# Casting weight loads one by one, replicated tables, and moved gating in a hybrid encoder kernel on eight cores

## What is computed

```python
def layer(x, c, ...):
    mod = jax.nn.silu(c) @ w_ada + b_ada                    # (B, 3D)
    shift, scale, gate = jnp.split(mod, 3, axis=-1)
    h = rmsnorm(x, norm_g) * (1.0 + scale[:, None, :]) + shift[:, None, :]
    z = h @ w_in                                            # (B, S, IN_WIDTH)
    a, ga, u, v, gb, ma, mb = jnp.split(z, IN_SPLITS, axis=-1)
    y_a = fourier_branch(a, w_fmix, b_fmix) * jax.nn.silu(ga)
    y_b = sgu_branch(u, v, sgu_ln_g, sgu_ln_b, w_s, b_s) * jax.nn.silu(gb)
    merged = jax.nn.sigmoid(ma) * (y_a @ w_pa) + jax.nn.sigmoid(mb) * (y_b @ w_pb)
    out = merged @ w_out
    return x + gate[:, None, :] * out
```

## Time and profile before

| what | value |
|---|---|
| median of 3 runs | 1265.08 us (1264.58 to 1265.36) |
| profiled execution | 1264.34 us |
| its span on the slowest core (core 4) | 1262.8 us |
| spans of the eight cores | 1249.7 to 1262.8 us |
| granted TensorE clock, mean per core | 0.984 to 0.991 of full |
| TensorE busy | 1203.5 us, 95% of the span |
| VectorE (DVE), ScalarE (ACT), GpSimd (POOL) busy | 700.2, 474.9, 318.8 us |

### The profile page before, as it was taken

The page is one execution under the profiler, slowest core; times in us unless marked ns, Lnnn a source line. Parts: engine busy times, 40 slices in busy tenths (PEclk is TensorE's granted clock), DMA queues, the critical chain, the costliest instruction groups (busy, mean ns, idle before and its releaser), DMA issues.

```text
span 1262.8 us, 19703 instructions; the slowest of 8 cores (1249.7 to 1262.8 us)
## 1 busy us (share of the span) xinstructions
PE 1203.5 (95%) x6128; PEld 564.2 (45%) x6128; DVE 700.2 (55%) x1133; ACT 474.9 (38%) x818; POOL 318.8 (25%) x406
## 2 busy tenths in 40 slices
PE   5799689999999999998999999999998999999997
PEld 0254344444444455545444444444443444444443
DVE  0384285554857668857556355445554663564544
ACT  1384232233323458845423432334232333332322
POOL 0131022461131232201721311312225413122111
PEclk9899899999999999999999999999999999999999
DMA  8999696325465278844430331413326315124121
GB/s 272 257 256 149 169 156 145 100 84 167 138 178 195 75 239 270 272 148 128 97 110 24 109 110 62 138 42 96 97 76 141 122 45 145 59 83 118 51 84 67
DMA packets 91123, 166.59 MB, mean 132 GB/s; under 512 B 39818, under 2 KB 52490, under 8 KB 89870
## 3 DMA queue, kind: packets, MB, share of 16 engines
q1 hardware_dynamic: 80606, 138.98, 35.4%
q0 software_dynamic: 9120, 17.96, 9.5%
q10 hardware_dynamic: 1296, 8.40, 2.0%
HBM read 143.41 MB, written 31.47 MB: 138 GB/s over the span
## 4 chain that ended last, share of the span: by engine, by line
PE 86%; DMA 8%; DVE 2%; POOL 1%; issue 1%; ACT 1%; ACTq 0%; SPq 0%; POOLq 0%; DVEq 0%
PE ps L702 43%; PE ps L621 13%; PE ps L814 6%; PE ps L820 6%; PE ps L505 6%; PE ps L712 5%; DMA arena<-w_ada 3%; DMA arena<-Gd 2%; PE ps L462 2%; DMA arena<-xA 1%; PE ps L515 1%; DMA Gd<-arena 1%; DMA arena<-xB 1%; PE ps L758 1%; PE ps L780 1%
## 5 line engine op out<-in xcount | busy, mean ns | idle before, releaser
L702 PE MATMUL ps<-arena 128*128 128x512 bf16 x2688 | 606.9, 381 | 5.4 <-ACT arena L806 3.5
L702 PEld LDWEIGHTS ps<-arena 128*128 128x128 bf16 x2688 | 262.7, 98 | 321.6 <-issue 16.5
L806 ACT ACTIVATE arena<-ps 128x512 bf16<-128x512 f32 x192 | 112.1, 595 | 243.4 <-PE ps L702 203.9
L825 POOL TENSOR_TENSOR arena<-arena 128x512 bf16<-128x512 bf16 x84 | 112.7, 1341 | 295.5 <-DVE arena L823 295.4
L621 PE MATMUL ps<-arena 128*128 128x512 bf16 x768 | 171.3, 379 | 0.4 <-DVE arena L823 0.4
L817 DVE TENSOR_TENSOR arena<-ps,arena 128x512 bf16<-128x512 f32 x96 | 66.2, 690 | 189.9 <-PE ps L814 187.5
L635 ACT ACTIVATE arena<-arena 128x1024 bf16<-128x1024 f32 x48 | 50.7, 1057 | 217.8 <-DVE arena L631 217.7
L408 POOL TENSOR_TENSOR stat<-stat,eps_sb 128x1 f32<-128x1 f32 (+1 forms) x114 | 28.8, 253 | 391.4 <-ACT arena L635 290.4
L421 ACT ACTIVATE arena<-arena 128x1024 bf16<-128x1024 f32 x96 | 101.3, 1055 | 69.0 <-DMA arena<-xB 45.5
L427 DVE TENSOR_SCALAR arena<-arena,stat 128x1024 bf16<-128x1024 f32 x96 | 84.7, 909 | 69.3 <-POOL stat L410 69.1
L621 PEld LDWEIGHTS ps<-arena 128*128 128x128 bf16 x768 | 75.1, 98 | 91.1 <-issue 1.5
(11 more groups left out here) (76 smaller groups left out, 930.6 us busy)
## 6 DMA issues: line engine op xcount, KB each, us to landing
arena<-xB SPq DMA_DIRECT2D x96, 512.0 KB, 4.5
arena<-xA SPq DMA_DIRECT2D x48, 512.0 KB, 6.8
yu<-arena SPq DMA_DIRECT2D x48, 512.0 KB, 2.8
arena<-w_ada SPq DMA_DIRECT2D x24, 512.0 KB, 5.2
arena<-w_in POOLq DMA_DIRECT2D x9, 1024.0 KB, 16.4
arena<-w_ada ACTq DMA_DIRECT2D x8, 1024.0 KB, 23.9
Gd<-arena SPq DMA_DIRECT2D x48, 128.0 KB, 5.4
arena<-Gd SPq DMA_DIRECT2D x12, 512.0 KB, 8.6
```

The source lines that it names most:

```text
L702: S.pe([lambda e, kc=kc: e.matmul(ps[b][:], lhsT=w_in_sb[:, sec, kc, col:col + 128], rhs=tb.hT[:, kc, :], start=(kc == 0), stop=(kc == 7)) ...
L806: S.op("act", lambda e, b=b, so=so: e.activation(out=bv(so, 512), in_=ps[b][:], func=AF.Sigmoid), reads=[("ps", b)], writes=gk(so, 1024))
L825: S.op("pool" if dmc < 7 else "dve", lambda e: e.tensor_tensor(out=tb.mg[:, dmc, :], in0=tb.mg[:, dmc, :], in1=bv(sl[1], 512), op=ALU.add) ...
```

## The change

1. `w_sec(0)` waits for chunk 5 of `w_ada` in place of 6, and the loads of x chunks 4 to 7 for chunk 6 in place of 7. In the first pass `sc(3)` moves behind the first projection's cast. The last `stage1` of a pass (`flush`) moves behind the next tile's transposes (first pass) or behind the first V group of tile 4 (second pass).
2. Sections 3 and 5 leave `hooks1`: section 3 is issued after V of tile 0, section 5 after GB of tile 0, `w_pab` after GB of tile 1, section 7 after U of tile 1. To say "after", the matmul groups now also write a key `("sec", sec)` that the casting DMA reads.
3. `b_adaG`, `ln_b`, `b_s` and `final_g` come as 128 equal rows in memory in place of one row that is read 128 times. `s3_begin(1)` comes ahead of `late_tabs`.
4. `sgu` moves behind `ga_section` in tiles 0, 1 and 4; `z_tr(1, ..)` of tile 5 moves from GA to GB; `w_out`'s products alternate between POOL and DVE and start one round later.
5. The very last `out_chunk` takes squares, scaling and store in halves of 512 columns.

```diff
@@ start and casts
-    w_sec(0, after=gk(wada_off[6], 512))
+    w_sec(0, after=gk(wada_off[5], 512))
...
-        3: lambda: (w_sec(4, after=[("aq", 1, 15)]), w_s_load(), w_sec(3), w_sec(5)),
+        3: lambda: (w_sec(4, after=[("aq", 1, 15)]), w_s_load()),
...
-    A.load_to(8, after=gk(wada_off[7], 512))
+    A.load_to(8, after=gk(wada_off[6], 512))
...
-    A.sc(3)
-    A.body(hooks1)
+    A.body(hooks1, late=True)
@@ groups
     def fm_group(tb, sec, col):
...
-             reads=gk(tb.h, 8192) + wink[sec], writes=[("ps", b)])
+             reads=gk(tb.h, 8192) + wink[sec], writes=[("ps", b), ("sec", sec)])
...
-                 reads=gk(tb.h, 8192) + wink[SEC["V"]], writes=[("ps", b)])
+                 reads=gk(tb.h, 8192) + wink[SEC["V"]], writes=[("ps", b), ("sec", SEC["V"])])
@@ tiles 0 and 1
+    A.fe(5)
+    A.flush()
+    s3_begin(1)
     late_tabs()
-    s3_begin(1)
-    A.fe(5)
-    for tb in pair:
-        v_section(tb)
+    v_section(T0)
+    w_sec(3, after=[("sec", SEC["V"])])
+    v_section(TB1)
     silu_section(T0, SEC["GB"], T0.sgb, T0.b)
+    w_sec(5, after=[("sec", SEC["GB"])])
     silu_section(TB1, SEC["GB"], TB1.sgb, TB1.b, lambda fc: s3s(0) if fc == 3 else None)
+    w_pab()
     u_section(T0, lambda fc: s3s(1 + fc // 2) if fc % 2 else None)
     channel_tables()
     w_sec(6)
-    w_pab()
-    w_sec(7)
+    u_section(TB1, lambda fc: s3s(3) if fc == 1 else None)
+    w_sec(7, after=[("sec", SEC["U"])])
     w_sec(8)
-    u_section(TB1, lambda fc: s3s(3) if fc == 1 else None)
-    for tb in pair:
-        sgu(tb)
-    w_out_load()
     final_tab()
     gate_load(0, 0)
     gate_load(1, 1)
     ga_section(T0, 0, 0, lambda fc: z_tr(1, fc))
+    sgu(T0)
     ga_section(TB1, 0, 1)
+    sgu(TB1)
+    w_out_load()
@@ products of w_out with the gate
-        S.op("pool", lambda e: e.tensor_tensor(out=w_out_sb[:, k, :], in0=w_out_sb[:, k, :], in1=fv(off, 1024), op=ALU.mult),
+        S.op(("pool", "dve")[k % 2], lambda e: e.tensor_tensor(out=w_out_sb[:, k, :], in0=w_out_sb[:, k, :], in1=fv(off, 1024), op=ALU.mult),
...
-    mul_order = ((0, 1), (2, 3), (4,), (5,), (6,), (7,), (), ())
+    mul_order = ((), (0, 1), (2, 3), (4, 5), (6, 7), (), (), ())
@@ tiles 4 and 5
-        v_section(tb)
+        v_section(tb, (lambda: (A2.flush(), s3_begin(0))) if T == 4 else None)
...
+            if T == 5:
+                z_tr(1, fc)
...
-        sgu(tb)
+        if T != 4:
+            sgu(tb)
...
-        ga_section(tb, u, t, (lambda fc: z_tr(0, fc)) if T == 4 else (lambda fc: z_tr(1, fc)) if T == 5 else None)
+        ga_section(tb, u, t, (lambda fc: z_tr(0, fc)) if T == 4 else None)
+        if T == 4:
+            sgu(tb)
@@ last chunk, in out_chunk
+            if last:
+                S.op("act", lambda e, half=half: e.activation(
+                    out=bv(O_XSR + 6144 + 1024 * half, 512), in_=xv[:, half * 512:(half + 1) * 512], func=AF.Square, scale=0.03125,
+                    accum_out=stat[:, 0, si + half:si + half + 1]),
+                    reads=hk, writes=[("st", si + half)] + gk(O_XSR + 6144 + 1024 * half, 1024))
+                if half == 0:
+                    finish()
```

More of the change, by code:

```diff
@@ L613, in finish, with out_chunk @@
             fins.pop(0)()
-    def out_chunk(tb, T, j, k, split=False):
-        si = stat2(1)
+    def out_chunk(tb, T, j, k, split=False, last=False):
+        si = stat2(2 if last else 1)
         row0 = T * 512 + j * 128
@@ L633, in out_chunk @@
                 reads=[("ps", b)] + hk, writes=hk)
+            if last:
[5 more added lines that the diff above has]
+                    finish()
+        if last:
+            S.op("dve", lambda e: e.scalar_tensor_tensor(out=stat[:, 1, si:si + 1], in0=stat[:, 0, si:si + 1], scalar=EPS,
+                                                         in1=stat[:, 0, si + 1:si + 2], op0=ALU.add, op1=ALU.add),
+                 reads=[("st", si), ("st", si + 1)], writes=[("st1", si)])
+            S.op("pool", lambda e: e.tensor_tensor(out=stat[:, 1, si:si + 1], in0=stat[:, 1, si:si + 1], in1=mh_sb[:, 0:1], op=ALU.pow),
+                 reads=[("st1", si), "mh"], writes=[("st1", si)])
+            for half in range(2):
+                hs = slice(half * 512, (half + 1) * 512)
+                hk = gk(XS[k] + 2048 * half, 2048)
+                S.op("dve", lambda e, hs=hs: e.scalar_tensor_tensor(out=xv[:, hs], in0=xv[:, hs], scalar=stat[:, 1, si:si + 1],
+                                                                    in1=fg_bc[:, hs], op0=ALU.mult, op1=ALU.mult),
+                     reads=hk + [("st1", si), "fg"], writes=hk)
+                out_tokens.append(S.dma("sp", [lambda e, hs=hs: e.dma_start(out=yu.ap()[row0:row0 + 128, hs], in_=xv[:, hs])],
+                                        "s_st%d" % (k if half else (k + 2) % 4), reads=hk, writes=[("yout", row0, half)]))
+            return
         jo = O_TYB if T in (0, 1, 3) else O_XSR + 6144
@@ L886, in body @@
                     if j % 2 == 0:
+                        if late and q == 0 and j == 0:
+                            self.sc(3)
                         self.sc(2 * q + j // 2 + 4)
```

35 lines of the change are left out of this document (18 added, 17 removed).

## The result

The kernel after takes **1272.43 us** (median of 5 runs, 1270.64 to 1273.28) against 1265.36 (5 runs, 1264.58 to 1266.77) for the kernel before on the same chip: a ratio of **1.0053**, 95% interval 1.0038 to 1.0068. That is slower by 7.1 us, where 1270 was forecast, 5 us slower. In some executions the cores of one half of the chip run at a lower granted clock and the time is longer; all medians and ratios here leave those out. The profiled execution took 1272.06 us, with a span of 1270.2 on core 4, the slowest core before too; the spans compared, 1270.2 - 1262.8, give 7.4.

The account below looks back on a forecast made before the run. TensorE bounds the kernel (86% of the chain). Terms: +15.1 to the end of U of tile 1, gating -5.4, tile 4 -1.5, tile 5 0, tile 8 -3.1: +5.1 on 1264.34, about 1270 us with the median's 0.7; range 1266 to 1275.

Parts of the forecast that it names:

- section 3: V of tile 1: TensorE waits 17.5 us for this w_in cast, landing at about 121.5; bounds 14.4 and 21.
- Section 5: GB of tile 1: TensorE waits 11.7 us for this w_in cast to land; bounds 7 and 16.4.
- The old wait: L575, after GB of tiles 0 and 1: TensorE's wait of 11.8 us for Gd goes.
- The start: First pass: earlier x loads and sc(3) behind the cast -3.3, flush behind the transposes -0.6; V of tile 0 at 97.1.
- The restarts: After TensorE's waits: 1.6 us at low clock for each, two in place of one, +1.6; bounds 0 and 3.2.
- Gating, tiles 0 and 1: Spatial gating moved beside GA and the sigmoid groups: -5.4 us, leaving 2 us for late banks; bounds -7.4 and -2.
- Tile 4: Waits of 1.28 and 1.1 us go, 0.9 is given back by the Fourier table: -1.5; bounds -2.4 and +1.
- Tile 5: Channel products moved from GA to GB: 4.2 us won, +3.9 from banks still held, net 0; bounds -4.2 and +2.
- Tile 8: Products on two engines, one round later, end TensorE's waits for sigmoids behind POOL: -3.1 us; bounds -3.5 and 0.
- The last chunk: End of the kernel: halves save 0.5 us on ACT, finish() puts a scaling ahead; 0, bounds -1 and +1.
- the fast casts: Rival, chance 0.11: awaited casts land at their queue's pace, two waits together under 21.5 us, sum 8.0 lower, 1262.
- The crowded casts: Rival, chance 0.10: section 3 lands as before less the shift (+3.5), section 5 meets other transfers (16.4, +4.8): 1278 us.

Follow-up runs that it names:

- the casts late: Kernel after, no group waiting for a cast's landing, and sections 5, 6, w_pa and w_pb called behind the channel tables: 1243.05 us, ratio 0.9826.
- the kernel with the old products: Kernel with the casts late, but w_out's products all on POOL in their old places: 1244.44 us, ratio 0.9853.
- the start alone: Kernel before with only the earlier first cast and x loads, the fourth scaling behind the cast, flush behind the transposes: 1262.99 us, ratio 0.9999.
- tiles 4 and 5 alone: Kernel before with only tile 4's Fourier first step, flush and gating moved and tile 5's channel products in GB: 1262.52 us, ratio 0.9975.
- the casts alone: Kernel before with only sections 3, 5 and 7 cast behind matmul groups, reading their key, and w_pa, w_pb behind GB of tile 1: 1290.45 us, ratio 1.0201.
- one-row tables and late casts: Kernel with the casts late, but ln_b, b_s, b_adaG and final_g again one row in memory: 1249.69 us, ratio 0.9873.

## Why the prediction was right

**The new waits.** The price of section 3 was 17.5 us, measured 16.0 on core 4 and 15.3 to 19.7 over the cores. Its landing was put at 121.5 and came at 119.2: issued 0.9 earlier than reckoned, and 13.3 us on the way, nearer to the lone cast of the earlier trace rows than to the crowded one. Section 5 was priced at 11.7 and took 12.6 (9.0 to 13.0). Here the Trainium skill's rule ("DMA: Bandwidth & Descriptors", "Anatomy of one DMA") had given an estimate of 6.8 us from issue to landing; the measured 11.84 us, with no other queue moving a packet, is against it, as the earlier trace rows was, and so are all eight cores (8.2 to 12.2). That these waits are what the change costs is shown by the kernel without them (-13 us) and by the one with the casts late (-29).

**The old wait.** Gone: the last load of `Gd` lands at 125.2 and TensorE asks for it at 155.9. The reason that the prediction gives for the old wait, the casts, is only a part of it, as the table above shows. The start gave -4.8 where -3.9 was reckoned (3.1 to the transposes, then 1.7 because the matmuls behind them run at full clock, which stood in the bounds only). The restarts cost 1.86 and 1.31 us, the old one 1.63: +1.5, forecast +1.6. The end of U of tile 1 moved by +13.5 where **+15.1** was forecast.

**Gating, tiles 0 and 1.** -5.4 forecast; -4.9 in the trace (-4.5 to -5.7 over the cores), -5.1 alone. The forecast left 2 us for banks that come free late; the rows show 1.65 and 0.25.

**Tile 4** was mis-sized, -1.5 against -4.3 (-2.5 to -4.4 over the cores, mean -3.2). The wait that was to give back 0.9 is there and is larger: TensorE waits 2.02 us for `Gd` at L550. The channel products won their 2.4, as worked (2.3). What had no term is the rest. `flush` between the groups of V saves 1.0. In the kernel before, a string of short waits for evictions stood in GB, and its last group ran at the lower clock behind them (8 matmuls in 3.39 us instead of 1.89); in the kernel after most of that is gone, and GB and U together are 1.5 us shorter even with the 2.02 in them. The gating costs 0.6 at the first merge round. I had priced only the waits that the change removes in GA.

**Tile 5** came out nearly as worked, 0 forecast and +0.9 measured (+0.7 to +2.5 over the cores), through the mechanism named: the products in GB wait for V's banks.

**Tile 8.** -3.1 forecast. Core 4 of the one profile shows +0.3, but over eight cores the waits fall from a mean of 3.8 us to 1.5 and the tile's share of the shift is -2.9 in the mean, and the kernel with the old products is 3.4 us slower. The size is right, though not on the core that the sum was made for; what I overlooked is that the products stand in DVE's order behind `w_out`'s load, and ACT's squares behind x loads, so that a core with a late load still waits. A DVE product took 1.23 us while POOL stood all but idle and 2.17 us beside POOL's tensor operations; a POOL product takes 2.13 and took 3.12 where it began 1.1 us before that DVE product ended. The Trainium skill's "SBUF — State Buffer", "Who interferes with whom", says that such a pair shuts each other out; each is longer by about the overlap, which agrees with it.

**Tile 3** was in no term: +2.3 us for a merge round behind DVE, which 14 us earlier had waited 6.64 us for a load of `w_ada` (4.34 in the kernel before). It need not be the change's. The kernels with the start alone and with tiles 4 and 5 alone, whose code there is that of before, show the same wait on 6 and on all 8 cores (0.4 to 2.4 us), and the kernel before on one (1.0).

**The last chunk** 0 forecast; -0.15 in the trace, 0.0003 in the ratios of the kernels with and without the halves.

The sum was 2.3 us too low on the profiled core: section 3, the start and section 5 together 1.6 too high, tile 4 2.8 and the end 0.4 too high; tile 8 3.4, tile 3 2.3, tile 5 0.9 and the gating 0.5 too low. So the mechanism and the two large prices are right, and the nearness of the total is partly luck: 4.8 us of misses on one side met 7.1 on the other. There is luck in the core, too. The sum takes off 11.8 us for `Gd`, the longest such wait of the eight; with the mean of 8.1 and the mean start of -2.8 the same working gives +9.9, and the mean span grew by 9.4. Of the rivals, the fast casts needed the two waits under 21.5 us; they are 28.6 on the slowest core and 24.6 or more on every core. The crowded casts needed 21 and 16.4; no core had either.

## What to carry to other kernels

A key that makes a DMA wait for a matmul group also makes the next writer of that key wait for the DMA. Where only the one direction is wanted, wait once and don't register as a reader. Then look who stands beside whom: freeing the casts of their waiters won 13 us, and holding `w_pa` and `w_pb`, due only at the merge, until the tables due sooner were read won another 16. The order of calls on one queue is not an order in time: a cast that is called behind another engine's work waits for it only if a key says so, and the trace shows which one did. And a win ahead of a stage that is owed a transfer can be given back at that transfer and at later ones: the start alone won 2.8 us in the mean and nothing in the time.

## What was not expected of the hardware

The issue of a DMA can itself last long. In the kernel before, SP spent 26.50 us on core 4 on the four loads of `Gd` (20.8 to 26.5 over the cores), and with the start alone 23.46 us on core 0, 0.39 us on the shortest of them and 10.8 on the longest. With section 5 gone from the queue it is 13.6 to 17.8 us (the casts alone), with the tables behind `Gd` 7.0 to 10.8 (the late casts), with both 3.9 to 8.9 (the kernel after). The timeline of SP with the start alone:

```profile
106.83 23.46 SPq L538 DMA_DIRECT2D arena<-Gd  x4
```

Whatever stands behind such a load on SP goes out later, small tables too: `cosC`, 64 KB, behind `Gd`, was under issue for 13.9 us in the kernel with one-row tables and late casts and for 6.8 in the one with the late casts. Why an issue lasts so long, no run here shows.
